# Filler products on TensorE ahead of its waits in a two-layer encoder kernel

## The chip, the cores and the metric

The kernel runs on one core of a Trainium2 chip. The metric is the device time of one execution in microseconds (us), lower is better. TensorE is written PE, VectorE DVE, ScalarE ACT, GpSimd POOL and SyncE SP, as in the profile. The profile also gives the clock that was granted to PE, as a share of full speed: its two levels are 1.2 GHz (0.50) and 2.4 GHz (1.00).

## What is computed

Two layers of a streaming encoder on 256 tokens of width 1024, all in float32, cut to its steps:

```python
for l in range(2):
    h = rmsnorm(x, mix_norm[l])
    proj = h @ w_in[l]                       # all branches at once
    q_g, k_g, v_g, z_g, a_g, b_g, c_q, c_kv, k_r, gate = split(proj)
    o_a = gdn_branch(...) @ w_gdn_o[l]       # gated DeltaNet, chunks of 64
    o_b = mla_branch(rmsnorm(c_q), rmsnorm(c_kv), ...) @ w_mla_o[l]
    x = x + (sigmoid(gate)[0] * o_a + sigmoid(gate)[1] * o_b) @ w_out[l]
    h2 = rmsnorm(x, ffn_norm[l])
    if l == 0: x = x + swiglu(h2, dense_w1, dense_w3, dense_w2)   # hidden width 3584
    else:      x = x + moe_ffn(h2)           # router, top 2 of 8 experts of width 1792
return rmsnorm(x, final_norm)
```

## The kernel before, in words

Every engine has its own program, written out by hand; semaphores tie them together, and each engine works through its program in order. There is no planner: the order of the lines is the order of the work.

**Weights.** SP loads the weights tile by tile into eight raw slots (a tile is 128 rows of a weight matrix, or two times 128 in the dense layer). A product in float32 is made from three faster ones: ACT rounds a tile to fp32r (`whi`, L531), DVE takes the rest (`wlo`, L864), in four slots each, and PE adds hi x hi, hi x lo and lo x hi (`prod`, L1404 to L1406). A slot of `whi` and `wlo` comes free when PE has used its tile (`w_used`), a raw slot when DVE has split it (`w_lo`). Tokens are taken as two blocks t of 128.

**A norm** n (0 and 2 ahead of the mixers, 1 and 3 ahead of the dense layer and the experts, 4 at the end). ACT squares and sums `x` (L544), POOL makes 1/rms (L456, L457), DVE writes the normalized rows to `hbuf` (L913). PE waits for `norm_h`, transposes eight 128 x 128 pieces into banks 4 and 5 for t = 0 and 6 and 7 for t = 1 (`norm`, L1450; the transposes are recorded at L1447), ACT rounds them to `aT_hi` (L556), DVE takes `aT_lo` (L927), and the products of the next stage wait for `norm_lo`. Between these steps ACT and DVE split the first tiles of the next stage.

**A mixer** begins with eight tiles `g1` (`by_token`, columns for the two latents, decay and rotary key), then eight tiles `z`. Ahead of z tile 5 PE transposes the two latents (`lat`), which DVE has normalized (L949, L950); ACT copies them to `pT_hi` (L592), DVE takes `pT_lo` (L984, semaphore `lat_lo`), and after z tile 7 PE waits for `lat_lo` and goes on with the two tiles `wkv` and three `wq`. The rest of the mixer (qkv tiles, attention, DeltaNet with its inversion by doubling, gates, output) is not touched. Its sums of squares are 16 products with one column each, recorded as 32 (L1596).

**The router** (layer 1, after norm 3). ACT copies the transposes to `h2T` (L558); PE makes the logits, 16 float32 products of eight columns, recorded as 32 (L1814), once `router_w` has landed (loaded by POOL, L440). ACT and DVE split `hbuf` to `h2_hi` and `h2_lo` (L798, L1288), DVE clears `y_hi` and `y_lo` (L1290, L1291), copies the logits (L1298), picks the two largest and makes the mask (`lg_ready`). PE makes each token's place in its expert's list (L1819 to L1823), DVE the ranks and the flag (`rank_ready`), then the selection matrix `sel` (L1324, `sel_ready`). PE clears two banks with products on zeros (L1849) and gathers the tokens of the first expert (`gather`, L1832), first from `h2_hi`, then, when ACT has copied that (`gat_hi`, L806), from `h2_lo`. Then the loop over eight experts, 48 tiles each.

What sets the order around the change is PE's own program: each wait of it holds everything behind it, and nothing of another engine is reordered. The PSUM has eight banks of 512 columns. In the norms, at the latent rows' wait and in the router up to the experts no engine reads or writes banks 2 and 3 at the places that the change touches.

Of the kernel before, what the change touches and what calls it, by code (L numbers as in the profile page):

```python
# [28 lines left out]
P = 128  # L29
# [53 lines left out]

def program(nc, A, out):
    _, T, D = A["x"].shape
    L, _, IN = A["w_in"].shape
    TT = T // P
    KC = D // P
# [48 lines left out]
    with st:  # L137
        def sb(name, shape, dt=F32, ctx=st):
            return ctx.enter_context(nc.sbuf_tensor(name, shape, dt))
# [14 lines left out]
        ident_r = sb("ident_r", [P, P], F32R)  # L154
# [138 lines left out]
        ps = st.enter_context(nc.psum_tensor("ps", [P, 8, 512], F32))  # L293

        def two(b):

            return ps[:, b:b + 2, :].rearrange("p a b -> p (a b)")
# [1101 lines left out]
        def _(pe):  # L1399
            mm = nc.tensor.matmul  # L1400
# [7 lines left out]
            def tile(t, n, c0=0):  # L1408
                pe.wait_ge(w_lo, t.count(1))
                sl = t.c % SPL  # L1410
                return whi[:, sl, c0:c0 + n], wlo[:, sl, c0:c0 + n]
# [33 lines left out]
            def transposes(o, src, n, w=P):  # L1445
                for k in range(n):
                    last = nc.tensor.transpose(o[0:w, k * P:(k + 1) * P], src[:, k * w:(k + 1) * w], ident[:, :])  # L1447
                return last

            def norm(n):  # L1450
                for t in range(TT):
                    pe.wait_ge(s["norm_h"], TT * n + t + 1)
                    transposes(two(4 + 2 * t), hbuf[:, t, :], KC).then_inc(s["norm_T"], 1)

            pe.wait_ge(s["ident_ready"], 1)

            for l in range(L):
# [13 lines left out]
                for j in range(KC):  # L1471
# [11 lines left out]
                        last = prod(ps[:, 4 + t, :], aT_hi[:, j, sl], aT_lo[:, j, sl], whs, wls, j == 0, j == KC - 1)  # L1483
                    last.then_inc(w_used, 1)

                pe.wait_ge(s["lat_lo"], TT * (l + 1))
                kv = (pT_hi[:, QC:LC, :], pT_lo[:, QC:LC, :])
                by_token(base, "wkv", 0, LC - QC, kv, [512, 512], 0)
# [119 lines left out]
                for t in range(TT):  # L1608
                    for j in range(2):
                        for h in range(H):  # L1610
                            o = ps[:, 4 + 2 * j + t, h * P:(h + 1) * P]
                            last = mm(o, gcol[:, 2 + j, t, h:h + 1].to_broadcast([P, P]), ident[:, :],
                                      start=True, stop=True)
                    last.then_inc(s["row_done"], 1)
                gate_tiles(7, 1)
                for t in range(TT):
                    pe.wait_ge(s["eq_in"], TT * l + t + 1)
                    sl = slice(t * P, (t + 1) * P)
                    for h in range(H):
                        mm(ps[:, 4 + t, h * P:(h + 1) * P], qk[:, H + h, sl], qk[:, H + h, sl], start=True, stop=True)  # L1620
                        last = mm(ps[:, 6 + t, h * P:(h + 1) * P], qk[:, H + h, sl], qk[:, h, sl],
                                  start=True, stop=True)
# [55 lines left out]
                for c in range(4):  # L1678
                    t, r = c // 2, slice((c % 2) * CHUNK, (c % 2 + 1) * CHUNK)
# [21 lines left out]
                    for h in range(H):  # L1701
                        hs = slice(h * P, (h + 1) * P)
                        if c:
                            mm(ps[r, 6 + t, hs], qdT[:, h, tk], S[:, 1 - c % 2, hs], start=True, stop=False)  # L1704
                        last = mm(ps[r, 6 + t, hs], inT[r, t, h * P + r.start:h * P + r.stop], vnb[r, t, hs],  # L1705
                                  start=(c == 0), stop=True)
# [33 lines left out]

                if l == 0:
                    norm(1)

                    def hidden_T(i, d, b):
# [62 lines left out]
                else:  # L1807
# [3 lines left out]
                    for t in range(TT):  # L1811
                        pe.wait_ge(s["norm_hi"], TT * 3 + t + 1)
                        for k in range(KC):
                            last = mm(ps[:, 0, t * NE:(t + 1) * NE], h2T[:, k, t * P:(t + 1) * P], rw[:, k, :],  # L1814
                                      start=(k == 0), stop=(k == KC - 1))
                    last.then_inc(s["lg_done"], 1)

                    pe.wait_ge(s["lg_ready"], 1)
                    mm(ps[:, 1, 0:NE], upper[:, :], mask[:, 0, :], start=True, stop=True)  # L1819
# [2 lines left out]
                    for t in range(TT):  # L1822
                        last = mm(ps[:, 1, 2 * NE:3 * NE], ones[:, :], mask[:, t, :], start=(t == 0), stop=(t == 1))  # L1823
                    last.then_inc(s["rank_done"], 1)
                    pe.wait_ge(s["rank_ready"], 2)

                    def gather(c, e, k):

                        src = (h2_hi, h2_lo)[k]
                        for f in range(KC):  # L1830
                            for t in range(TT):
                                last = mm(two(6)[:, f * P:(f + 1) * P], src[:, t, f * P:(f + 1) * P],  # L1832
                                          sel[:, t, :], start=(t == 0), stop=(t == TT - 1))
                        last.then_inc(s["gat_done"], 1)

                    def scatter(t, bank=6):

                        for b in range(2):
                            sl, cs = slice(t * P, (t + 1) * P), slice(b * 512, (b + 1) * 512)
                            mm(ps[:, bank + b, :], selT[:, sl], y_hi[:, cs], start=True, stop=False)  # L1840
                            last = mm(ps[:, bank + b, :], selT[:, sl], y_lo[:, cs], start=False, stop=True)  # L1841
                        last.then_inc(s["sct_done"], 1)

                    def experts(base, r):
                        pe.wait_ge(s["sel_ready"], 18 * r + 2)
                        if r == 0:

                            for b in range(2):
                                mm(ps[:, 4 + b, :], selT[:, 0:P], y_hi[:, b * 512:(b + 1) * 512], start=True, stop=True)  # L1849
                        gather(18 * r, None, 0)  # L1850
                        pe.wait_ge(s["gat_hi"], 18 * r + 1)
                        gather(18 * r, None, 1)
                        with pe.Fori(0, NE) as e:
                            def halves(c):
                                return At(8 + 16 * r + c, e, 2).count()

                            def pairs(c):
                                return At(18 * r + c, e, 2).count()

                            pe.wait_ge(s["gat_hi"], pairs(2))  # L1860
                            for j in range(4 * KC):
                                wi, hf, k = (j // KC) % 2, j // (2 * KC), j % KC
                                if j == 6:

                                    pe.wait_ge(s["ey_lo"], At(9 * r + 1, e, 1).count())
                                    scatter(0)
                                if j == 9:
                                    pe.wait_ge(s["sct_used"], pairs(1))
                                    scatter(1)
                                if j == 12:  # L1870
                                    pe.wait_ge(s["sct_used"], pairs(2))
                                    for t in range(TT):
                                        last = mm(ps[:, 6, t * P:(t + 1) * P], sel[:, t, :], ident_r[:, :],
                                                  start=True, stop=True)
                                    last.then_inc(s["selT_done"], 1)
                                if j == 16:
                                    pe.wait_ge(s["h1_used"], halves(1))
                                if j == 20:
                                    pe.wait_ge(s["selT_used"], At(8 * r + 1, e, 1).count())
                                    pe.wait_ge(s["h3_used"], halves(1))  # L1880
                                    transposes(two(6), ehid[:, 0:HC], EC // 2).then_inc(s["hT_done"], 1)
                                whs, wls = tile(At(base + j, e, N_EXP), HC)
                                for b in range(2):
                                    cs = slice(b * HC // 2, (b + 1) * HC // 2)
                                    last = prod(ps[:, 2 * wi + b, 0:HC // 2], gT_hi[:, k, :], gT_lo[:, k, :],
                                                whs[:, cs], wls[:, cs], k == 0, k == KC - 1)
                                last.then_inc(w_used, 1)

                            pe.wait_ge(s["sel_ready"], pairs(4))
                            pe.wait_ge(s["hT_lo"], halves(1))  # L1890
                            gather(0, e, 0)
                            j = 4 * KC
                            for k in range(EC):
                                if k == 3:
                                    pe.wait_ge(s["gat_hi"], pairs(3))
                                    pe.wait_ge(s["h3_used"], halves(2))
                                    transposes(two(6), ehid[:, HC:FE], EC // 2).then_inc(s["hT_done"], 1)
                                if k == EC // 2:
                                    pe.wait_ge(s["hT_lo"], halves(2))
                                if k == 10:  # L1900
                                    gather(0, e, 1)
                                for b in range(2):
                                    halved = k >= EC - 2
                                    T_ = At(base + j, e, N_EXP)
                                    if b == 0 or halved:
                                        whs, wls = tile(T_, D if not halved else D // 2)
                                    cs = slice(0, 512) if halved else slice(b * 512, (b + 1) * 512)
                                    last = prod(ps[:, 4 + b, :], eT_hi[:, k, :], eT_lo[:, k, :],
                                                whs[:, cs], wls[:, cs], k == 0, k == EC - 1)
                                    if b == 1 or halved:  # L1910
                                        last.then_inc(w_used, 1)
                                        j += 1
                            assert j == N_EXP
# [33 lines left out]
```

## Time and profile before

| | us |
|---|---|
| median of three timed runs | 1415.92 |
| lowest and highest | 1413.58 to 1417.61 |
| span of the profiled execution (its only time given) | 1420.8 |
| PE busy in it | 1330.4 (94%) |
| DVE busy | 956.9 (67%) |
| ACT busy | 817.5 (58%) |
| share of the chain that ended last on PE | 86% |
| mean granted clock | 0.966 |

The span is that of one execution under the profiler. Busy PE is not PE at its peak, as matmuls overlap: a 512-column product is shown as 0.39 us long, but the next one starts 0.23 us later. The clock line is read as tenths of full speed for each fortieth of the span. The first clock record of this trace lies 19.16 us after the span's start; before it the column shows 1.00 and has nothing to go by.

### The profile page before, as it was taken

What the parts mean: (1) busy time and instruction counts of PE and PEld (TensorE: products, weight loads), DVE (VectorE), ACT (ScalarE), POOL (GpSimd) and SP (SyncE); (2) the same over time, 40 slices, a digit from 0 to 9 for tenths busy, and PEclk for the clock granted to TensorE, in tenths of its full rate; (3) what the DMA queues carried; (4) which work ended last, traced back from release to release, by engine and by line L of the source; (5) the groups of instructions that cost most, each with busy time, mean ns of one, the idle gap of its engine ahead of it and who ended that gap; (6) DMA issues with size and microseconds to landing.
All of it is one profiled execution on the core that took longest, in us unless ns stands there. A gap on an engine that the chain in (4) does not pass through costs nothing.

```text
span 1420.8 us, 20371 instructions
## 1 busy us (share of the span) xinstructions
PE 1330.4 (94%) x7066; PEld 1156.8 (81%) x7066; DVE 956.9 (67%) x1221; ACT 817.5 (58%) x1057; POOL 62.3 (4%) x114
## 2 busy tenths in 40 slices
PE   6999999989999998999999978999999999999996
PEld 5798787779999787799787767888888888989794
DVE  5657755655555444557755747888979797979795
ACT  4567423344444333567522427787878787878784
POOL 2800001000000001000000000000000000000000
PEclk9999999989999998998999968999999999999998
DMA  7544212556666453644122507998989898989892
GB/s 244 159 152 136 73 60 75 163 157 176 187 180 198 152 163 106 200 128 140 57 75 63 180 25 252 327 325 315 328 314 324 315 329 319 336 314 343 302 346 100
DMA packets 98971, 289.06 MB, mean 203 GB/s; under 512 B 10241, under 2 KB 26625, under 8 KB 98913
## 3 DMA queue, kind: packets, MB, share of 16 engines
q1 hardware_dynamic: 97168, 282.70, 59.6%
q0 software_dynamic: 1744, 5.60, 1.4%
q8 instruction: 36, 0.59, 0.2%
q14 instruction: 23, 0.18, 0.0%
HBM read 287.20 MB, written 1.05 MB: 203 GB/s over the span
## 4 chain that ended last, share of the span: by engine, by line
PE 86%; DVE 8%; issue 3%; ACT 2%; DMA 1%; POOL 1%; ACTq 0%; DVEq 0%; POOLq 0%
PE ps L1404 24%; PE ps L1406 23%; PE ps L1405 23%; PE ps L1832 2%; PE ps L1447 2%; DVE wlo L864 2%; PE ps L1666 1%; PE ps L1665 1%; PE ps L1705 1%; PE ps L1526 1%; PE ps L1546 1%; PE ps L1642 1%; PE ps L1704 1%; PE ps L1840 1%; PE ps L1841 1%
## 5 line engine op out<-in xcount | busy, mean ns | idle before, releaser
L864 DVE TENSOR_TENSOR wlo<-raw,whi 128x896 fp32r<-128x896 f32 (+4 forms) x614 | 650.1, 1087 | 279.9 <-ACT whi L531 275.9
L531 ACT ACTIVATE whi<-raw 128x896 fp32r<-128x896 f32 (+4 forms) x614 | 572.7, 949 | 286.6 <-PE ps L1406 281.9
L1404 PE MATMUL ps<-whi,aT_hi 128*128 128x448 f32 (+2 forms) x544 | 212.0, 390 | 10.0 <-DVE wlo L864 5.9
L1405 PE MATMUL ps<-wlo,aT_hi 128*128 128x448 f32 (+2 forms) x544 | 207.8, 382 | 0.0
L1406 PE MATMUL ps<-whi,aT_lo 128*128 128x448 f32 (+2 forms) x544 | 207.7, 382 | 0.0
L1404 PE MATMUL ps<-whi,gT_hi 128*128 128x448 f32 x512 | 192.4, 376 | 14.2 <-DVE wlo L864 13.7
L1406 PE MATMUL ps<-whi,gT_lo 128*128 128x448 f32 x512 | 187.8, 367 | 0.0
L1405 PE MATMUL ps<-wlo,gT_hi 128*128 128x448 f32 x512 | 187.4, 366 | 0.0
L1404 PEld LDWEIGHTS ps<-whi,aT_hi 128*128 128x128 f32 x544 | 105.9, 195 | 27.5 <-DVE wlo L864 6.7
L1404 PEld LDWEIGHTS ps<-whi,gT_hi 128*128 128x128 f32 x512 | 96.6, 189 | 33.6 <-DVE wlo L864 26.0
L1406 PEld LDWEIGHTS ps<-whi,aT_lo 128*128 128x128 f32 x544 | 105.5, 194 | 16.1
L1405 PEld LDWEIGHTS ps<-wlo,aT_hi 128*128 128x128 f32 x544 | 106.0, 195 | 14.7
L1405 PEld LDWEIGHTS ps<-wlo,gT_hi 128*128 128x128 f32 x512 | 96.8, 189 | 7.9
L1406 PEld LDWEIGHTS ps<-whi,gT_lo 128*128 128x128 f32 x512 | 96.5, 188 | 8.1
L1404 PE MATMUL ps<-whi,eT_hi 128*128 128x512 f32 x224 | 90.0, 402 | 0.0
L1405 PE MATMUL ps<-wlo,eT_hi 128*128 128x512 f32 x224 | 88.4, 395 | 0.0
L1406 PE MATMUL ps<-whi,eT_lo 128*128 128x512 f32 x224 | 88.4, 395 | 0.0
L1404 PE MATMUL ps<-aT_hi,whi 128*128 128x256 f32 x192 | 55.8, 290 | 0.0
L1405 PE MATMUL ps<-aT_lo,whi 128*128 128x256 f32 x192 | 54.3, 283 | 0.0
L1406 PE MATMUL ps<-aT_hi,wlo 128*128 128x256 f32 x192 | 54.3, 283 | 0.0
L725 ACT ACTIVATE Lm<-ps 128x512 f32<-128x512 f32 x20 | 11.9, 597 | 67.0 <-PE ps L1642 67.0
L1406 PEld LDWEIGHTS ps<-whi,eT_lo 128*128 128x128 f32 x224 | 42.0, 187 | 10.2
(360 smaller groups left out, 1838.2 us busy)
## 6 DMA issues: line engine op xcount, KB each, us to landing
raw<-in_moe_w SPq DMA_DIRECT2D x256, 448.0 KB, 4.7
raw<-in_moe_w SPq DMA_DIRECT2D x96, 512.0 KB, 6.5
raw<-in_dense_w SPq DMA_DIRECT2D x64, 448.0 KB, 3.6
raw<-in_w_in SPq DMA_DIRECT2D x32, 512.0 KB, 3.9
raw<-in_dense_w SPq DMA_DIRECT2D x28, 512.0 KB, 4.3
raw<-in_w_in SPq DMA_DIRECT2D x32, 384.0 KB, 3.9
raw<-in_w_out SPq DMA_DIRECT2D x16, 512.0 KB, 4.5
raw<-in_moe_w SPq DMA_DIRECT2D x32, 256.0 KB, 3.2
```

The lines of the kernel that those rows point to most:

```text
L531: a(whi[:, t.c % SPL, 0:n], raw[:, t.c % RAW, 0:n], ACT.Copy).then_inc(w_hi, 1)
L864: tt(wlo[:, t.c % SPL, 0:n], raw[:, t.c % RAW, 0:n], whi[:, t.c % SPL, 0:n].bitcast(F32), ALU.subtract).then_inc(w_lo, 1)
L1404: mm(o, hi, rhi, start=start, stop=False, skip_group_check=skip)
L1405: mm(o, hi, rlo, start=False, stop=False, skip_group_check=skip)
L1406: return mm(o, lo, rhi, start=False, stop=stop, skip_group_check=skip)
L1447: last = nc.tensor.transpose(o[0:w, k * P:(k + 1) * P], src[:, k * w:(k + 1) * w], ident[:, :])
L1526: last = mm(two(3)[:, h * nk:(h + 1) * nk], qT[:, hh, t * P:(t + 1) * P], kT[:, hh, 0:nk], start=True, stop=True)
L1546: last = mm(ps[:, 7, (h0 + h) * VD:(h0 + h + 1) * VD], probT[:, u % 2, c * P:(c + 1) * P], vm[:, k, (h0 + h) * VD:(h0 + h + 1) * VD], star ...
L1642: last = mm(ps[:, 4 + t, hs], MT[:, t, hs], X[:, t, hs], start=True, stop=True)
L1665: mm(ps[:, 6, hs], XT[:, t, hs], Lm[:, t, hs], start=True, stop=True)
L1666: last = mm(ps[:, 7, hs], Lm[:, t, hs], XT[:, t, hs], start=True, stop=True)
L1832: last = mm(two(6)[:, f * P:(f + 1) * P], src[:, t, f * P:(f + 1) * P], sel[:, t, :], start=(t == 0), stop=(t == TT - 1))
```

## The change

PE gets a helper `keep(n, bank)`, which issues n products of the identity (`ident_r`, fp32r, 128 x 128) with the identity read four times over (512 columns) into one bank that nothing reads. It is called ahead of waits: in `norm` ahead of the wait for t = 0 (20 times a product in the first norm, 11 in the others) and for t = 1 (6), and 5 behind the last transposes; 12 ahead of the wait for `lat_lo` in each layer; 12 behind the logits; 6 behind the ranks; 5 between the two gathers of the first expert; 18 ahead of the loop over the experts (`experts(OVER, 1)` is for more than 128 tokens on one expert and does not run here). Nothing is taken away.

```diff
+            def keep(n, bank):
+
+                for _ in range(n):
+                    mm(ps[:, bank, :], ident_r[:, :], ident_r[:, :].unsqueeze(1).to_broadcast([P, 4, P]),
+                       start=True, stop=True)
+
             def norm(n):
                 for t in range(TT):
+                    keep((20 if n == 0 else 11) if t == 0 else 6, 2 + t)
                     pe.wait_ge(s["norm_h"], TT * n + t + 1)
                     transposes(two(4 + 2 * t), hbuf[:, t, :], KC).then_inc(s["norm_T"], 1)
+                keep(5, 2)
...
                     last.then_inc(w_used, 1)
 
+                keep(12, 2)
                 pe.wait_ge(s["lat_lo"], TT * (l + 1))
...
                     last.then_inc(s["lg_done"], 1)
+                    keep(12, 2)
 
                     pe.wait_ge(s["lg_ready"], 1)
...
                     last.then_inc(s["rank_done"], 1)
+                    keep(6, 2)
                     pe.wait_ge(s["rank_ready"], 2)
...
                         gather(18 * r, None, 0)
+                        keep(5, 2)
                         pe.wait_ge(s["gat_hi"], 18 * r + 1)
                         gather(18 * r, None, 1)
+                        keep(18, 2)
                         with pe.Fori(0, NE) as e:
```

## Rows read from the trace of the kernel before

**Rows 1.** The page: the clock line, and the chain that ended last by engine.

```profile
PEclk9999999989999998998999968999999999999998
...
PE 86%; DVE 8%; issue 3%; ACT 2%; DMA 1%; POOL 1%; ACTq 0%; DVEq 0%; POOLq 0%
```

**Rows 2.** Stretches: bounds, length, busy us (instructions) by engine, granted clock, DMA share, GB/s.

```profile
294.88:299.05 4.17, 4.17 (x11) 3.78 (x12) 2.13 (x2) 0.71 (x1) 0.00 (x0) 0.50 0.62 212
...
552.80:558.46 5.66, 5.66 (x18) 4.80 (x18) 2.00 (x2) 0.94 (x2) 0.00 (x0) 0.50 0.72 227
...
828.13:862.25 34.12, 23.08 (x94) 21.56 (x95) 14.33 (x42) 13.06 (x14) 0.02 (x1) 0.50 0.13 40
...
928.26:996.49 68.23, 66.82 (x332) 58.21 (x332) 58.01 (x58) 53.78 (x59) 0.00 (x0) 1.00 0.92 323
```

**Rows 3.** Waits of PE from 40 to 90 us: total, times, longest.

```profile
PE ps L1404 <- DVE wlo L864: 3.3, 1, 3.3
```

**Rows 4.** Timeline of the start: start, length, instruction, in brackets idle before and releaser.

```profile
2.20 0.28 DVE L877 CAST ident_r<-ident 128x128 fp32r<-128x128 f32 x1
...
11.14 3.85 PE L1447 MATMUL ps<-ident,hbuf 128*128 128x128 f32 x16 [11.14 <-DVE hbuf L913]
...
12.88 1.65 DVE L864 TENSOR_TENSOR wlo<-raw,whi 128x680 fp32r<-128x680 f32 x2
...
15.71 0.79 PE L1404 MATMUL ps<-whi,aT_hi 128*128 128x512 f32 x1 [0.73 <-DVE aT_lo L927]
```

**Rows 5.** Chain that ended last: start, length, what; products at both clocks, and small ones.

```profile
128.60 3.58 PE ps L1596 x32
...
136.65 0.43 PE ps L1406
...
139.00 0.23 PE ps L1406
...
665.64 4.63 PE ps L1596 x32
...
903.02 1.74 PE ps L1832 x16
```

**Rows 6.** Timeline of the second norm.

```profile
288.66 1.86 PE L1447 MATMUL ps<-ident,hbuf 128*128 128x128 f32 x8 [2.51 <-DVE hbuf L913]
...
291.59 2.10 DVE L864 TENSOR_TENSOR wlo<-raw,whi 128x896 fp32r<-128x896 f32 x2
291.73 1.97 PE L1447 MATMUL ps<-ident,hbuf 128*128 128x128 f32 x8 [1.21 <-DVE hbuf L913]
...
294.88 0.74 PE L1404 MATMUL ps<-whi,aT_hi 128*128 128x448 f32 x1 [1.18 <-DVE aT_lo L927]
```

**Rows 7.** Timeline around the wait for the latent rows, first layer.

```profile
49.35 2.46 DVE L864 TENSOR_TENSOR wlo<-raw,whi 128x1024 fp32r<-128x1024 f32 x2
...
51.55 0.39 PE L1404 MATMUL ps<-whi,pT_hi 128*128 128x512 f32 x1
```

**Rows 8.** Timeline of the fourth norm, the router and the first gather.

```profile
825.74 1.09 PE L1447 MATMUL ps<-ident,hbuf 128*128 128x128 f32 x8 [2.51 <-DVE hbuf L913]
...
831.00 7.00 PE L1814 MATMUL ps<-rw,h2T 128*128 128x8 f32 x32 [1.05 <-DMA rw<-in_router_w]
...
835.58 0.91 DVE L1291 MEMSET y_lo<- 128x1024 f32 x1 [0.16 <-issue]
...
838.03 0.17 DVE L1298 COPY lg<-ps 128x16 f32<-128x16 f32 x1 [1.23 <-PE ps L1814]
...
840.89 0.60 PE L1819 MATMUL ps<-mask,upper 128*128 128x8 f32 x2 [2.90 <-DVE tw L1308]
...
844.67 1.19 PE L1849 MATMUL ps<-y_hi,selT 128*128 128x512 f32 x2 [1.48 <-DVE sel L1324]
...
850.29 3.67 PE L1832 MATMUL ps<-sel,h_lo 128*128 128x128 f32 x16 [1.11 <-ACT gT_hi L806]
...
858.46 0.74 PE L1404 MATMUL ps<-whi,gT_hi 128*128 128x448 f32 x1 [4.50 <-DVE wlo L864]
```

## The prediction

> **What bounds the kernel now.** I read the page first: TensorE (PE) carries 86% of the chain that ended last, and the clock line is at nine tenths or more but for a few dips [rows 1]. So what counts is PE's own time, its waits, and how fast it runs behind them. Then I asked for stretches with the granted clock. After three of the four norms PE's first products run at 0.50 of full speed, 1.2 GHz: 4.17 us of them at the first layer's second norm, 5.66 us at the second layer's first; from 828.13 to 862.25 (router, first gather, first products of the experts) everything does [rows 2]. For the first norm the trace has no clock record before 19.16 us; the first product there, at 15.71, lasts 0.79 us [rows 4], so I read those 3.45 us as 1.2 GHz too. Last I read the timeline for what precedes each: a wait of 2.51 us for the normalized rows, eight transposes, a wait of 1.2 us, eight more, and a wait for aT_lo or, at the router, for router_w [rows 6, 8]. PE is idle or transposing for some six microseconds and comes out at half speed. A product of 512 columns takes 0.43 us at 1.2 GHz and 0.23 us at 2.4 GHz [rows 5].
>
> **The price of a filler.** The change removes and moves nothing; it adds 162 products on PE's queue, each into bank 2 or 3, which no engine reads meanwhile. One costs what a product of 512 columns does, so the price is 0.23 us at 2.4 GHz, 0.43 at 1.2; its 128 x 128 weights are of the same shape and its 512 columns are the same count. Reading one 128-column block four times might be cheaper or dearer; no row shows it, and I take the product. The Trainium skill, "TensorE: Matmul & The Clock Gate", section "Back-to-back issue gap", gives about 131 ns for a sustained 512-column product with its weight load; the trace disagrees, with 0.23 us at full clock. By the page every figure for fillers below would be little over half, and the sum some 2.4 us better at the latent rows.
>
> **First norm (start).** PE has ident_r at about 2.5 us and waits until 11.14 [rows 4]. Twenty fillers last 8.6 us if all run at 1.2 GHz: they end at 11.1, so they hide at either clock. I expect the clock to be up well before. Then six fillers (1.4 us) stand ahead of the second transposes: eight transposes take 1.09 us at full clock [rows 8], so these start at about 13.6, 0.6 late, and end at 14.7, sooner than before. Five more (1.15 us) end at 15.8 against a first product at 15.71, which is set by VectorE: its two wlo splits from 12.88 and then aT_lo [rows 4]. Cost 0.1. The 3.45 us of products at half clock become 1.7. Gain 1.6; bounds -3.6 (fillers all slow: 2.2 late at the second transposes, then 2.1 more ahead of the products) and 1.8.
>
> **Second norm (294.88).** Eleven fillers, 2.5 us, fill the 2.51 wait exactly. Six, 1.4 us, follow transposes of 1.09 from 288.66 and end at 291.1, before the wait ends at 291.73. Five end at 294.0, before 294.88; that start stays, since VectorE splits two tiles from 291.59 until 293.6 and only then makes aT_lo [rows 6]. So only the clock counts: 4.17 us at half speed, gain 2.1. **Third norm:** the same shape, 5.66 us, gain 2.8 [rows 2]. These two are bounded by nothing gained, and by a loss of 2.3 us each if the fillers run at 1.2 GHz. The next tiles are ready: splits take about 1.1 us a tile, PE over 2 us.
>
> **Latent rows.** Twelve fillers stand ahead of the wait for lat_lo, after the last z tile, in both layers. PE does not wait there: between 40 and 90 us its only wait on VectorE's splits is 3.3 us ahead of a z tile, five tiles earlier in that loop [rows 3]. VectorE's lat_lo is done when it turns to the next two splits at 49.35; the first is done at about 50.6, and PE comes at 51.55 and goes on without a gap [rows 7]. So the fillers are plain added work: 12 x 0.23 = 2.8 us, twice, 5.5 us lost. PE is the bound from there on, and nothing gives it back. The idle 3.3 us gets no filler. Bounds: 0 (cheap fillers, or a wait that I don't see) to 10.3 (both at 1.2 GHz).
>
> **Router and first gather** [rows 8]. The logits wait for router_w until 831.0 whatever the fillers do. At 1.2 GHz their 32 products take 7.0 us. Thirty-two products of the same kind with one column take 3.58 us, and 4.63 where the clock fell under them [rows 5]; I take 4.2 for the logits, bounds 3.6 and 7.0. But VectorE is next: it splits h2 and clears y_hi and y_lo until 836.5 to 836.8 and only then copies the logits (838.03). With the second transposes 0.7 us sooner this queue ends at 836.1. So the logits give 1.9 us, not 2.8. Then twelve fillers stand against a wait of 2.90 us: 2.8 us at full clock. Such one-column products did bring the clock down in the mixers, so I expect it to fall under the logits and the twelve to take up to 5.1 us, from 835.2 to 840.3; this returns 1.3 of the 1.9 where it falls early. I take a gain of 1.2 here. The fillers then bring the clock back. The ten ranking products, 2.3 us, would take 1.4 (gain 0.9); six fillers, 1.4 us, hide in the wait of 1.48; the two products ahead of the gather give 0.5. The gathers take 3.5 and 3.7 us from their starts; in the loop at full clock sixteen such products take 1.74 [rows 5]: gains 1.8 and 1.9. Five fillers (1.15) stand against 1.11. Eighteen take 4.1 us against the 4.50 in which ScalarE copies, loads a table and splits, and VectorE splits: hidden. The first expert lasts from 858.46 to 928.26, 69.8 us, the next 68.2 [rows 2]: started at full clock it gains 1.6. No wait in the experts is for a transfer that these gains could run into: PE is busy in 66.8 of 68.2 us. Sum 7.9; 0.3 off for a second fall among the waits. **7.6.** Bounds: -7.5 to 10.
>
> **Sum:** 1.6 + 2.1 + 2.8 + 7.6 - 5.5 - 0.1 for the small overruns = 8.5 us less. Of the profiled execution only its span is given, 1420.8 us; its like would span 1412.3. The median of the three timed runs is 1415.92, 4.9 us below the profiled span; taken off it, 1407.4.
>
> **Rivals.**
> 1. *Fillers outlast their waits at half clock* (slower). The clock falls under the logits and stays down. Twelve cost 5.1 against 2.9, six 2.6 against 1.5, five 2.1 against 1.1, eighteen 7.7 against 4.5: 7.5 lost at the router, 1.6 won at the first expert. With the norms' 6.5 and the latent 5.5: 4.9 slower, 1420.8. For it: the fall under such products is in the trace. Against it: fillers without a gap are what the norms' products are, and behind those the clock rose every time. It decides once the twelve and the six both run slow. Chance 0.10.
> 2. *The router gives only a part* (no change). The clock is back only under the eighteen; they overrun a little, and gathers or ranking stay slow. Router gain 2 to 3, in all 3 less, 1413. Chance 0.18.
> 3. *Transposes undo the fillers.* Before the falls at the norms PE ran transposes between its waits, and the clock was down at their end [rows 6, 8]. The Trainium skill, "TensorE: Matmul & The Clock Gate", Part 4, says that transposes do not count as busy in the way products do; by that rule a norm might still come out slow. Here the fillers of such a norm (six and five at 0.43) would make the first products 2.3 us late and keep them slow: norms 3.6 + 2.3 + 2.3 lost, latent 5.5 lost, router as in rival 1 without the gain: some 22 slower, 1438. Against it: after the change products stand between the transposes, and behind products the clock rose. Chance 0.04. That identity products do not raise the clock at all ends at the same time; it is counted here.
> 4. *The latent fillers are free*, and all else holds: 14 less, 1402. Chance 0.06.
>
> **Numbers.** The forecast has 0.62, with a range of its own of 1403 to 1412: router 5 to 9.5, the start 0 to 1.8, and one or two of the untouched dips of the clock more or fewer, 1.7 us each. A measurement of this kernel tells 0.3% (4.2 us) from no change. Faster: the forecast but for its upper edge (0.58), rival 4 (0.06), a little of rival 2 (0.03): 0.67. Slower: rivals 1 and 3, 0.13. The same: 0.20. The range of 1402 to 1417 leaves out rivals 1 and 3 and the ends.
>
> **What would show it.** In the profile after: the clock at 1.00 in the first products behind the first three norms; no fall between 288 and 299 and between 548 and 558; PE's first product behind each norm not later than before; twelve filler rows of 0.23 us ahead of wkv with no wait behind them, and the stretch from the last z tile to wkv 2.8 us longer; logits near 4.2 us, lg copied near 5 us after the logits' start; the clock low for less than 10 us between the logits and the experts instead of 34; the gathers at 1.74. Wrong would be filler rows of 0.43 us with their waits gone, or a clock that falls in spite of them.

## The result, and the profile after

Over 20 runs each, the changed kernel takes 1413.34 us in the median (1407.24 to 1418.3) against 1418.73 for the kernel before (1413.58 to 1422.64): ratio 0.9961, 95% interval 0.9947 to 0.9974, that is 5.5 us less (3.7 to 7.5). The sign was forecast; the size was not: 8.5 less was forecast, and 1407.4 us. Two parts make up the 5.9 us by which that number is off: 2.8 because the three runs that it started from lie below the median of twenty, and 3.1 because the change gives less than the 8.5 us of its sum.

The profiled execution after spans 1414.2 us. First the clock line of its page and the chain by engine, against [rows 1]:

```profile
PEclk9998999999999999999999999999999999999998
...
PE 86%; DVE 8%; issue 3%; ACT 2%; DMA 1%; POOL 1%; ACTq 0%; DVEq 0%; POOLq 0%
```

The dips at the norms and the long one at the router are gone from the line. The stretches behind the three norms, then the router, with the columns of [rows 2]:

```profile
297.42:301.60 4.18, 4.18 (x21) 3.88 (x22) 2.08 (x2) 0.00 (x0) 0.00 (x0) 1.00 0.65 209
552.32:557.98 5.66, 5.66 (x32) 4.94 (x33) 2.23 (x3) 1.03 (x3) 0.00 (x0) 1.00 0.65 226
832.16:838.97 6.81, 6.81 (x25) 6.04 (x25) 5.39 (x22) 0.98 (x2) 0.00 (x0) 0.50 0.00 0
838.99:852.54 13.55, 13.21 (x79) 10.83 (x77) 3.63 (x16) 5.47 (x6) 0.00 (x0) 1.00 0.00 1
```

In 4.18 us behind the second norm PE now starts 21 products where it started 11, in 5.66 us behind the third 32 instead of 18. From the router on the clock is low for 6.8 us, not 34. The second norm's first product still waits for VectorE, against [rows 6]:

```profile
297.42 0.47 PE L1404 MATMUL ps<-whi,aT_hi 128*128 128x448 f32 x1 [0.89 <-DVE aT_lo L927]
```

The start of the kernel, against [rows 4]:

```profile
2.53 6.50 PE L1453 MATMUL ps<-ident_r 128*128 128x512 f32 x20 [2.53 <-DVE ident_r L877]
...
11.71 1.64 PE L1453 MATMUL ps<-ident_r 128*128 128x512 f32 x6
...
13.98 1.40 PE L1453 MATMUL ps<-ident_r 128*128 128x512 f32 x5
...
15.54 0.50 PE L1404 MATMUL ps<-whi,aT_hi 128*128 128x512 f32 x1 [0.16 <-DVE aT_lo L927]
```

Twenty fillers take 6.5 us, so the clock rose under them, and the first product lasts 0.50 us instead of 0.79. The latent rows, against [rows 7]:

```profile
47.61 2.46 DVE L864 TENSOR_TENSOR wlo<-raw,whi 128x1024 fp32r<-128x1024 f32 x2
...
49.77 2.89 PE L1453 MATMUL ps<-ident_r 128*128 128x512 f32 x12
...
52.50 0.39 PE L1404 MATMUL ps<-whi,pT_hi 128*128 128x512 f32 x1
```

VectorE's lat_lo was done at 47.6 and the first split at 48.8, before the first filler: 2.7 us from the last z product to wkv for nothing. The router, against [rows 8]:

```profile
830.17 5.23 PE L1823 MATMUL ps<-rw,h2T 128*128 128x8 f32 x32 [0.33 <-DMA rw<-in_router_w]
...
835.25 4.74 PE L1453 MATMUL ps<-ident_r 128*128 128x512 f32 x12
835.45 0.17 DVE L1298 COPY lg<-ps 128x16 f32<-128x16 f32 x1
...
839.83 0.28 PE L1829 MATMUL ps<-mask,upper 128*128 128x8 f32 x2
...
843.02 1.90 PE L1843 MATMUL ps<-sel,h_hi 128*128 128x128 f32 x16
...
847.87 4.32 PE L1453 MATMUL ps<-ident_r 128*128 128x512 f32 x18
```

The logits take 5.2 us: the clock fell 2 us into them. VectorE's clearing ends at 835.5, just as they do, and the copy follows at once. The twelve fillers, at half clock until 838.97, outlast their wait: the mask is ready at 838.3 and the ranks start at 839.83. From there ranks, gathers and the first expert's products run at full clock.

### The profile page after: what moved, and what is told of

Same layout as the page of the kernel before. It is cut to its first block, busy times and chain, and to the rows that moved or that the text cites. A ratio compares the mean times of both kernels' runs of the same rounds, so it can differ in the third digit from the quotient of the medians.

```text
span 1414.2 us, 20694 instructions
## 1 busy us (share of the span) xinstructions
PE 1352.6 (96%) x7228; PEld 1174.0 (83%) x7228; DVE 955.7 (68%) x1221; ACT 817.1 (58%) x1057; POOL 62.3 (4%) x114
## 4 chain that ended last, share of the span: by engine, by line
PE 86%; DVE 8%; issue 3%; ACT 2%; DMA 1%; POOL 1%; ACTq 0%; DVEq 0%; POOLq 0%
PE ps L1404 24%; PE ps L1406 23%; PE ps L1405 23%; PE ps L1843 2%; PE ps L1447 2%; DVE wlo L864 2%; PE ps L1675 1%; PE ps L1674 1%; PE ps L1453 1%; PE ps L1714 1%; PE ps L1535 1%; PE ps L1555 1%; PE ps L1851 1%; PE ps L1651 1%; ACT whi L531 1%
## 5 line engine op out<-in xcount | busy, mean ns | idle before, releaser
L1406 PEld LDWEIGHTS ps<-whi,eT_lo 128*128 128x128 f32 x224 | 42.0, 187 | 10.2
```

The lines of the kernel that those rows point to most:

```text
L1406: return mm(o, lo, rhi, start=False, stop=stop, skip_group_check=skip)
```

## Experiments

Each was timed against the kernel before on the same chip in five rounds, unless said. The changed kernel's clock also dips where nothing was changed (behind the z wait, under the sums of squares, at the end of a mixer), in other lengths in each trace; its three traces span 1414.2, 1406.3 and 1411.7 us.

**The parts alone.** e1 keeps only the fillers in the norms, e2 only those at the latent rows, e3 only those in the router, the gather and ahead of the experts, e4 all but those at the latent rows. The edit of e4 against the changed kernel:

```diff
-                keep(12, 2)
                 pe.wait_ge(s["lat_lo"], TT * (l + 1))
```

> Only the fillers in the norms; none at the latent rows, none in the router and gather. Theory 1 (the parts add up as the two traces show: first norm 1.6 us, second 1.8, third 2.4, and about 1.8 at the fourth norm, because the second transposes and the logits start at full clock): 6 to 8 us faster than before, ratio about 0.995, and the low stretch from the fourth norm on starts under the logits and lasts into the experts. Theory 2 (the norms give less on the average of many runs than in this one pair of traces, since the low stretch behind them has a different length each time): 3 to 4 us faster.

> Only the twelve fillers at the latent rows in both layers. Theory 1: they hide nothing, 2.75 us each, so 5.5 us slower than before, ratio 1.004. Rival (they keep later dips of the clock away, or a later wait takes them in): within 2 us of before.

> Only the four calls in the router, the gather and ahead of the experts. The clock falls at the fourth norm as before, so the twelve run at half clock (5.1 us against a wait of 2.9) and bring it back. Theory 1: ranks, gathers and the first expert's products run at full clock; 5 us faster than before, less than the 7.2 of the two traces because the norm's share is missing. Rival (the twelve outlast their wait and the clock does not come back before the experts): 0 to 4 us slower.

> The change without the fillers at the latent rows. Theory 1: the change is 5.4 us faster than before on the median, and this adds the 5.5 us that those fillers cost: 11 us faster than before, ratio about 0.992. Rival (the fillers at the latent rows cost little, and the sum is small because norms and router give little): no more than 6 us faster than before.

| kernel | median, us | before | ratio (95%) | us |
|---|---|---|---|---|
| e1 norms | 1413.26 | 1418.36 | 0.9950 (0.9926 to 0.9974) | -7.1 |
| e2 latent | 1423.43 | 1418.36 | 1.0033 (1.0018 to 1.0048) | +4.7 |
| e3 router | 1412.67 | 1418.36 | 0.9965 (0.9940 to 0.9989) | -5.0 |
| e4 all but latent | 1407.02 | 1418.36 | 0.9914 (0.9889 to 0.9939) | -12.2 |

The us are the difference of the ratio from 1, times 1418.4. Each lies where its theory 1 put it, but e1's interval (3.7 to 10.5 us) reaches into theory 2 and e3's is as wide (1.6 to 8.5). Norms and router give 12.1 apart and 12.2 (8.7 to 15.8) together; the latent fillers cost 4.7 (2.6 to 6.8). Without them the change is worth about twice as much. e3 shows the router's fillers beginning with the clock already down and bringing it back (columns as above):

```profile
826.00:839.00 13.00, 11.60 (x47) 10.43 (x46) 6.91 (x23) 4.40 (x5) 0.00 (x0) 0.50 0.10 35
839.80:856.00 16.20, 15.85 (x91) 13.31 (x90) 6.76 (x19) 8.61 (x10) 0.00 (x0) 1.00 0.13 41
```

And e1, without them, keeps 0.51 for the whole way from 829 to 856:

```profile
829.00:856.00 27.00, 16.86 (x68) 15.65 (x68) 12.38 (x41) 8.86 (x10) 0.00 (x0) 0.51 0.12 38
```

**Fillers where PE does wait.** e5 is e4 with the following; the wait for `cw_ready` is there because ScalarE reads bank 7 until then:

```diff
+                    if j == 3:
+                        if l == 0:
+                            pe.wait_ge(s["cw_ready"], L)
+                        keep(13 if l == 0 else 10, 7)
                     whs, wls = tile(At(base + first["z"] + j), QW)
```

> The change without its fillers at the latent rows; in their place 13 (first layer) and 10 (second) into bank 7 ahead of z tile 3, where PE does wait, 3.3 and 2.6 us. Theory 1 (fillers ahead of a real wait cost nothing and keep the clock up behind it): no fall of the clock behind that wait, z products at 0.23 us; each fall there cost 1.7 us, so 1 to 3 us faster than the change without the latent fillers, 13 to 15 us faster than before. Rival (that fall is too short to matter, or the clock falls somewhere else instead): no difference to it, 12 us faster than before.

1406.27 against 1419.88, ratio 0.9909 (0.9881 to 0.9937), 12.9 us less. The fall behind that wait is gone from the trace. The first stretch here is e5's, the second the changed kernel's:

```profile
40.34:46.00 5.66, 5.66 (x30) 4.76 (x31) 4.09 (x6) 2.65 (x4) 4.92 (x10) 1.00 0.83 271
```

```profile
40.13:46.00 5.87, 5.87 (x24) 4.83 (x25) 2.80 (x4) 1.31 (x3) 5.09 (x11) 0.71 0.80 256
```

Thirty products start in 5.66 us, where 24 did in 5.87. One trace alone would not show that the fillers did it: of the 15 traces without them two have no fall behind this wait in the first layer either (e10 and e14), and six none in the second. With them (e5 and e11 below) it is absent in both layers of both traces. The timed runs are those of e4 within their interval, so the 1 to 3 us are not told by the times.

**Real work instead of fillers.** e7 is e4 with the sums of squares in two halves and a gate tile behind each:

```diff
                 for j in range(2):
...
+                    gate_tiles(4 + j, 1)
...
-                gate_tiles(4, 3)
+                gate_tiles(6, 1)
```

> The change without its fillers at the latent rows, and in each mixer the 16 one-column products of the sums of squares are split in two, with a gate tile of 2.8 us behind each half, so that real work stands between them instead of behind them. Theory 1 (those products bring the clock down in every mixer, for 7 to 10 us): the clock stays up there, 3 to 4 us gained in each layer, 6 to 8 us faster than the change without the latent fillers, 18 to 20 faster than before. Rival (the sums come 5.6 us later and the next step waits for them, 1 to 3 us a layer): no gain over 12 us.

1403.33 us, ratio 0.9886 (0.9861 to 0.9912): 16.2 less than before (12.5 to 19.7), 4 less than e4, somewhat under the 6 to 8 expected. The intervals of e4 and e7 overlap, so these two alone don't settle it. The clock over that stretch, in the kernel before and then in e7:

```profile
128.44:145.23 16.79, 16.79 (x85) 14.94 (x84) 10.07 (x26) 7.86 (x11) 0.00 (x0) 0.80 0.47 138
```

```profile
128.00:145.00 17.00, 17.00 (x110) 15.31 (x110) 10.19 (x25) 9.06 (x14) 0.00 (x0) 1.00 0.32 90
```

PE is busy without a break in both, and it starts 110 instructions where it started 85. The later sums made no wait: PE's waits in that mixer are those of before. Here the traces agree: all 15 without this edit have a fall under the sums of squares in both layers, and the two with it (e7, e11) have none in either.

**Fillers among the logits.** e8 is e4 with `keep(2, 2)` after every fourth logits product.

> The change without its fillers at the latent rows, and two fillers after every fourth logits product (six in all, 1.4 us), which the wait for VectorE's clearing of y_hi and y_lo should take in. Theory 1 (the logits, of eight columns, bring the clock down because PE streams little in them): the clock stays at 1.00 from the fourth norm to the experts and ranks come about 1 us sooner; 0.5 to 2 us faster than the change without the latent fillers, so 12.5 to 14 faster than before. Rival (six are too few, the fall stays and the logits are only longer): 0 to 1.4 us slower than without them.

1406.73 us, ratio 0.9908 (0.9875 to 0.9940): no different from e4. In its trace the clock still fell, and stayed down for 10.2 us, against 3.4 in e4's:

```profile
829.47:839.66 10.19, 10.19 (x36) 8.82 (x34) 4.30 (x21) 0.21 (x1) 0.00 (x0) 0.50 0.00 0
```

So six are too few, as the rival said. Whether they also cost time, the timed runs can't tell; in this trace the ranks start 12.2 us after the logits, in e4's 8.0.

**What a filler must be.** e9 is e4 with every filler of 512 columns replaced by two of 8:

```diff
-                for _ in range(n):
-                    mm(ps[:, bank, :], ident_r[:, :], ident_r[:, :].unsqueeze(1).to_broadcast([P, 4, P]),
-                       start=True, stop=True)
+                for _ in range(2 * n):
+                    mm(ps[:, bank, 0:8], ident_r[:, :], ident_r[:, 0:8], start=True, stop=True)
```

> The change without its fillers at the latent rows, every filler of 512 columns replaced by two of 8 columns with the same weights. PE is about as busy as with the wide ones: two gather products, the nearest in kind, take 0.22 us at full clock and 0.44 at half. Theory 1 (what keeps the clock up is the columns that PE streams, and a queue full of narrow products does not do it, as under the logits): the clock falls at every norm as before, the fillers run at 0.2 us each instead of 0.11 and outlast their waits, first products come up to 2.3 us late; slower than before by 5 to 20 us. Rival (any busy PE will do): the same as the wide fillers, 12 us faster than before.

1434.89 us against 1418.99, ratio 1.0101 (1.0084 to 1.0119), 14.3 slower. The timeline of its second norm:

```profile
289.73 2.51 PE L1453 MATMUL ps<-ident_r 128*128 128x8 f32 x22
292.40 1.09 PE L1447 MATMUL ps<-ident,hbuf 128*128 128x128 f32 x8 [0.16 <-DVE hbuf L913]
293.25 1.77 PE L1453 MATMUL ps<-ident_r 128*128 128x8 f32 x12
295.47 1.97 PE L1447 MATMUL ps<-ident,hbuf 128*128 128x128 f32 x8 [0.45 <-DVE hbuf L913]
297.09 2.27 PE L1453 MATMUL ps<-ident_r 128*128 128x8 f32 x10
299.22 0.72 PE L1404 MATMUL ps<-whi,aT_hi 128*128 128x448 f32 x1
```

PE is idle for 0.6 us in these ten, and the clock falls all the same: the second transposes take 1.97 us and the last fillers, at half clock, hold the products back. In all ten traces with wide fillers in these places, transposes and all, the first products behind the norms run at full clock. So a full queue was not enough; of the two kinds of filler only the wide one kept the clock.

**Together.** e11 has e4, e5 and e7.

> Together: no fillers at the latent rows, fillers at the z wait (e5), the sums of squares in two halves with a gate tile behind each (e7). Both of their gains are at different places, so they add: e5 took 13.6 us off the time before, e7 16.6, the change without the latent fillers 12.2; 17 to 19 us faster than before, ratio about 0.9875. Rival (the two overlap): no more than e7's 16.

1395.59 us (1394.88 to 1400.87) against 1418.99, ratio 0.9843 (0.9825 to 0.9860), 22.3 less (19.9 to 24.8): better than both kernels, and more than 17 to 19. It also settles what e7's times left open: e11 is e5 with the sums split, and takes 9 us more off than e5's 12.9 (8.9 to 16.9). Against e7 (12.5 to 19.7) it adds only the fillers at the z wait, 6 us more; these intervals only just part, and each falls on five or six runs.

**Why the sum was too large.** Six runs ask whether the sizes read from one trace hold. e6 and e14 are the changed kernel again; e10 and e12 the kernel before, one traced execution each; e13 the kernel before in twelve; e16 has only the fillers of the second and third norm. What was expected, in the order e6, e10, e12, e13, e14, e16:

> The changed kernel once more, unaltered, for a second trace and more timed runs. If the parts add up (norms 7.1, router 5.0, latent rows 4.7 lost, each against before in the median) it is 7.4 us faster than before, ratio 0.9948; if something in the whole is worse than its parts, it stays at 5.4 us, 0.9961. The dips of the clock that the change does not touch should lie at the same places and differ in length.

> The kernel before once more, for a second trace of it. Theory 1 (the execution of the first trace had longer low stretches than most: 13.3 us of products at half clock behind the first three norms, 1420.8 us of span): about 10 to 11 us behind the norms here, and a span nearer to 1416. Rival (they are as long each time): 13 us again, and a span of 1420.

> The kernel before a third time, for the same question: the low stretches lie behind the same waits and the length of each changes from execution to execution; 8 to 13 us of products at half clock behind the first three norms.

> The kernel before against itself. The ratio should be 1 within its interval. Theory A (profiled executions of this kernel are longer than its timed ones): the profiled one is again some 4 us above the timed median, near 1423. Theory B (three long ones by chance): it lies anywhere from 1414 to 1424.

> The changed kernel a third time. If the traced sum holds in the timed runs, 8 us less than before; if the two medians so far hold, 5.5 us less, ratio 0.996.

> Fillers at the second and the third norm alone. By the traces: 8.8 us of products at half clock are done at full clock, 4.4 us faster than before, ratio 0.9969. If the timed runs gain less than the traces show: 2 to 3 us, 0.998 to 0.9986.

e6: ratio 0.9959 (0.9944 to 0.9975). e14: 0.9976 (0.9956 to 0.9996). e13: 1.0004 (0.9986 to 1.0021). e16: 0.9980 (0.9965 to 0.9994), 2.8 less. Spans: e10 1421.0 and e12 1421.5, e13 1416.5 us; e6 1406.3 and e14 1411.7. Seven traces have no fillers at the first norm (the kernel before four times, e2, e3, e16), and six of them none at the second and third. The low stretches behind the second norm and the third in e10, e12, e2 and e3, in this order:

```profile
294.14:297.17 3.03, 3.03 (x8) 2.73 (x9) 2.13 (x2) 0.72 (x1) 0.00 (x0) 0.50 0.72 269
550.24:556.58 6.34, 6.34 (x20) 5.37 (x21) 2.00 (x2) 0.95 (x2) 0.00 (x0) 0.50 0.64 204
```

```profile
295.20:301.11 5.91, 5.91 (x16) 5.26 (x17) 2.13 (x2) 0.72 (x1) 0.00 (x0) 0.50 0.67 217
553.73:557.11 3.38, 3.38 (x10) 2.80 (x11) 2.00 (x2) 0.94 (x2) 0.00 (x0) 0.50 0.89 289
```

```profile
294.28:297.39 3.11, 3.11 (x8) 2.81 (x9) 2.14 (x2) 0.73 (x1) 0.00 (x0) 0.50 0.73 261
550.24:553.39 3.15, 3.15 (x9) 2.67 (x10) 2.00 (x2) 0.95 (x2) 0.00 (x0) 0.50 0.90 282
```

```profile
294.39:300.29 5.90, 5.90 (x16) 5.25 (x17) 2.14 (x2) 0.72 (x1) 0.00 (x0) 0.50 0.63 213
552.91:556.29 3.38, 3.38 (x10) 2.80 (x11) 2.00 (x2) 0.94 (x2) 0.00 (x0) 0.50 0.86 298
```

They are 3.0 to 5.9 and 3.2 to 6.3 us long: the length changes from execution to execution. With the first trace and e13 (4.19 and 3.14) their means are 4.4 and 4.2, against the 4.17 and 5.66 that the prediction had. Behind the first norm two of the seven have nothing at half clock; the first product of e13:

```profile
15.71 0.50 PE L1404 MATMUL ps<-whi,aT_hi 128*128 128x512 f32 x1 [0.73 <-DVE aT_lo L927]
```

So the first trace overstated the gain at the three norms, but by 1 us and no more. Was it a long execution as a whole? The other executions have no trace, but their times and mean granted clocks are on record:

| executions | number | mean time, us | mean granted clock |
|---|---|---|---|
| kernel before, traced (the first, e10, e12, e13) | 4 | 1421.8 | 0.9665 |
| kernel before, the others timed beside e1 to e16 | 88 | 1418.3 | 0.9689 |
| changed kernel, traced (the first, e6, e14) | 3 | 1412.6 | 0.984 |
| changed kernel, the others | 41 | 1413.5 | 0.9835 |

The time of an execution is its span and 1.8 us. By that the first trace's execution, 1422.6, is the longest of its twenty, and e10's and e12's (1422.8 and 1423.3) are longer than 85 of the 88. So e10 came out as its rival said, a span of 1420 again, and yet theory 1 was right that the first execution was a long one: e10 and e12 are long ones too. Over the 88, an execution is 1.1 us longer for each 0.001 less of clock, so the lower clock of the four answers for some 2.7 of their 3.5 us. By the traced executions the change is worth 9.2 us, by the others 4.8. In which stretches the others had the clock up for longer, no trace shows.

## Why the prediction was right or wrong

- *What bounds the kernel* was right: PE, its waits and its clock behind them. At the router the clock comes back before the experts when fillers stand there (e3) and does not without them (e1).
- *The price of a filler*, 0.23 us, was right: twelve in 2.89 us with the tail of the last, 2.7 from the first one's start to the next product's. The 131 ns of the Trainium skill ("TensorE: Matmul & The Clock Gate", "Back-to-back issue gap") does not hold here: 0.23 us at full clock.
- *First norm.* As worked out: the z wait is over at 40.13, before at 41.87, of which 0.17 is an earlier start of the products, so gain 1.6 in this pair. But where the clock is up by 15.7 without any filler there is nothing to gain, and two of seven executions are so. The means of the seven and of the traces with fillers give 1.3: mis-sized by some 0.3 us.
- *Second and third norm.* The mechanism held: no fall, and PE is idle for 0.9 and 0.5 us between the last filler and the first product, so the fillers don't set its start. Sizes by the mean of six traces: 2.2 and 2.1, not 2.1 and 2.8. The third norm's term is mis-sized by 0.7, because one length of a fall that lasts 3.1 to 6.3 us was taken for its size.
- *Latent rows.* Right: no wait there, and each set costs 2.7 us; alone they cost 4.7 (2.6 to 6.8), against 5.5. The prediction's rows show PE without a gap there for the first layer only; e2 bears out the sum of both.
- *Router.* Right in order and in size by the traces: from the end of the last output product to the first expert's product 35.2 us before, 29.8, 28.7 and 28.5 in the three traces of the changed kernel, and the experts' start at full clock. The fall under the logits, the twelve that outlast their wait and the recovery under them came as described, and VectorE's queue ended 5.3 us after the logits' start (forecast 5.1). In this trace the fall came early, the logits took 5.2 us, not 4.2, and the ranks started 9.7 us after the logits did (before 9.9, forecast 9.3 at most): 0.2 won there, not 1.2. In e6 and e14 the fall came later and they started 8.0 after: 1.9 won. The mean of the three, 1.3, is the forecast's 1.2.
- *The rivals.* Rival 1 was what e9 shows when fillers can't lift the clock: the route to a slower kernel was real, 14.3 us of it. Rival 2's number, 1413, is almost the one measured, and that is luck: what it supposed did not happen, since in all three traces the clock is back under the twelve, ahead of ranks and gathers, and by the traces the router gave its full part. Rival 3, that transposes undo the fillers, fell in every trace with wide fillers; what the Trainium skill says of transposes ("TensorE: Matmul & The Clock Gate", Part 4) changed nothing here. The terms of rival 3 add up to 21 us, not 22. Rival 4 fell with e2.
- *The sum, and the step that failed.* The waits, overlaps and paths of the sum held; its sizes failed. They were read from one execution of the kernel before, the longest of its twenty (its span 1420.8 us, clock 0.966). By the means of all traces the terms give 1.3 + 2.2 + 2.1 for the norms, some 8 for router and first expert, 5.4 lost: about 8, not 8.5. Timed, the change gives 5.5, 5.8 and 3.4 us in three sets of runs. e16 shows the same at a smaller scale: 4.4 expected of the traces, 2.8 (0.9 to 5.0) timed. Of the 3 us between forecast and timed, up to 1 is the norm terms. The rest has its counterpart in the table above: the traced executions of the kernel before took 3.5 us more than its others, at a lower clock, and those of the changed kernel 0.9 less. Sizes of falls that are read from them come out too large for the common execution. Which of the terms shrinks there, and why three of the four traced ones are that long, stays open.
- *Two explanations that the record does not bear out.* That tracing itself lengthens an execution is not what the other kernels show: of 13 traced executions of the changed kernel and the others tried, 8 are longer than the median of their kernel's others and 5 shorter, from 6.5 us less to 9.8 more. That the changed kernel gives something back in falls elsewhere is not what its traces show either: where nothing was changed the clock is low for 37.5, 20.5 and 37.5 us in them, for 30.7, 30.7, 34.1 and 30.7 in the four of the kernel before, 32 in the mean of each.
- *The base.* Three runs of the kernel before gave 1415.92; 20 gave 1418.73. Against a spread of 9 us a median of three is not known to better than a few us. This start, 2.8 us too low, is the other half of the error in 1407.4.

## What to carry to other kernels

Put fillers only ahead of waits that the trace shows, make them wide, and count them so that they end with the wait; ahead of no wait each is paid in full (2.7 us for twelve), and the two sets here cost about half of what the rest gained. Where many narrow products stand in a row, real wide products between them (e7, e11) kept the clock up and cost nothing; the few fillers tried in such a row (e8) did not keep it. And where a cost depends on a clock that falls at its own times, take its length from several executions, not from one, and compare the time and clock of the traced one with those of the others.

## What the runs showed of the hardware

The clock fell with PE's queue full. Under 32 one-column products without a gap (from 131.8 us in the kernel before), and among 22, 12 and 10 products of eight columns that, with the transposes, left PE idle for 0.6 us in ten (e9), it went to 0.50, as it does in the idle waits of 2.5 us at the norms. How long it stays there differs from execution to execution: 3.0 to 5.9 us of products behind the second norm. The fp32r products of 512 columns with the identity as both operands kept it at 1.00 at the norms in ten traces (e16's at two norms only), and 20 of them at the start brought it up: they take 6.5 us, where at half clock they would take 8.6. Two halves of eight one-column products, 1.84 us each with wide products between them, did not bring it down in either layer (e7, e11).
